# A norm's factor per token taken out of a matmul operand and put on the results, with regrouped convolution taps, in a two-block transformer kernel on one Trainium2 core

## The reference, cut to what matters

```python
def hybrid_layer(x, ...):
    h = rms_norm_2(x, norm_g)            # x * rsqrt(mean(x*x) + eps) per token, times norm_g per channel
    proj = jnp.einsum('bsd,dn->bsn', h, w_in)
    (q_a, k_a, v_a, o_a, i_a, f_a, z_a, c_q, c_kv, k_r, z_b, g_a, g_b) = jnp.split(proj, offsets, axis=-1)
    qk_a = jax.nn.silu(causal_depthwise_conv(jnp.concatenate([q_a, k_a], axis=-1), conv_w))   # 4 taps in time
    h_a = rms_norm(mlstm_chunkwise(q, k, v_a, i_a + gate_bias[:H_A], f_a + gate_bias[H_A:]))
    y_a = (jax.nn.sigmoid(o_a) * h_a * jax.nn.silu(z_a)) @ w_a
    q_b = rms_norm_2(c_q, q_lat_g) @ w_uq;   kv_b = rms_norm_2(c_kv, kv_lat_g) @ w_ukv
    o_b = causal_attention(...)          # k_r, rotated, is shared by all heads
    y_b = (o_b * jax.nn.silu(z_b)) @ w_b
    return x + (jax.nn.sigmoid(g_a) * y_a + jax.nn.sigmoid(g_b) * y_b) @ w_out
```

## Time and profile before

| | |
|---|---|
| time, median of 3 runs | 2551.07 us (2550.17 to 2552.93) |
| profiled execution, its own time | 2552.17 us |
| its span | 2550.4 us |
| mean granted TensorE clock | 0.997 |
| ACT busy | 1250.1 us, 49% |
| DVE busy | 1619.5 us, 63% |
| POOL busy | 146.2 us, 6% |
| chain that ended last | PE 94%, ACT 2%, DVE 2%, DMA 1% |
| loaded from HBM | 506.93 MB, 200 GB/s over the span |

### The profile page before, as it was taken

One profiled execution on the slowest core, in us unless ns is written; L12 is line 12 of the kernel. 1 busy time (PEld: TensorE's weight loads), 2 busy tenths in 40 slices (PEclk: granted clock), 3 DMA queues, 4 the chain that ended last, 5 costly groups with the idle time before them and its releaser, 6 DMA issues.

```text
span 2550.4 us, 34507 instructions
## 1 busy us (share of the span) xinstructions
PE 2514.2 (99%) x13608; PEld 2133.0 (84%) x13608; DVE 1619.5 (63%) x2365; ACT 1250.1 (49%) x1899; POOL 146.2 (6%) x148
## 2 busy tenths in 40 slices
PE   6999999999999999999999999999999999999999
PEld 2688899998888888888888888888888888888887
DVE  3576787886588886566665666665555554545554
ACT  3244433334465554355554555555566665544443
POOL 1001100010001110001110000001000000000000
PEclk8999999999999999999999999999999999999999
DMA  9953677775569885566665455555554555555555
GB/s 334 342 181 114 224 244 248 245 240 184 206 192 273 268 262 190 194 189 189 191 190 191 163 169 174 174 170 185 174 164 151 157 166 189 181 190 184 188 189 165
DMA packets 459104, 511.42 MB, mean 201 GB/s; under 512 B 36771, under 2 KB 327682, under 8 KB 458432
## 3 DMA queue, kind: packets, MB, share of 16 engines
q1 hardware_dynamic: 455936, 501.11, 61.9%
q0 software_dynamic: 2864, 8.11, 1.0%
q10 hardware_dynamic: 144, 0.02, 0.0%
HBM read 506.93 MB, written 2.22 MB: 200 GB/s over the span
## 4 chain that ended last, share of the span: by engine, by line
PE 94%; ACT 2%; DVE 2%; DMA 1%; issue 1%; SPq 0%; DVEq 0%; ACTq 0%
PE PG L926 17%; PE PG L928 17%; PE PG L927 17%; PE PG L916 13%; PE PG L919 6%; PE PG L935 4%; PE PG L937 4%; PE PG L936 4%; PE PS L831 1%; PE PS L1040 1%; ACT wh L1179 1%; PE PG L847 1%; DMA XC<-in_ctxT 1%; PE PS L1104 1%; PE PG L849 1%
## 5 line engine op out<-in xcount | busy, mean ns | idle before, releaser
L1576 DVE TENSOR_TENSOR wl<-raw,wh 128x1024 fp32r<-128x1024 f32 (+1 forms) x745 | 910.3, 1225 | 705.2 <-ACT wh L1179 703.3
L1179 ACT ACTIVATE wh<-raw 128x1024 fp32r<-128x1024 f32 (+1 forms) x745 | 785.9, 1057 | 863.1 <-PE PG L928 575.6
L916 PE MATMUL PG<-FHL,wh 128*128 128x512 f32 x1376 | 431.1, 397 | 2.4 <-DVE UP L1832 1.5
L926 PE MATMUL PG<-wh,HHL 128*128 128x512 f32 x832 | 331.3, 398 | 0.1
L928 PE MATMUL PG<-wl,HHL 128*128 128x512 f32 x832 | 324.9, 391 | 0.0
L927 PE MATMUL PG<-wh,HHL 128*128 128x512 f32 x832 | 324.3, 390 | 0.0
L919 PEld LDWEIGHTS PG<-FHL,wl 128*128 128x128 f32 x1376 | 256.3, 188 | 59.4
L919 PE MATMUL PG<-FHL,wl 128*128 128x256 f32 x1376 | 267.9, 278 | 0.0
L916 PEld LDWEIGHTS PG<-FHL,wh 128*128 128x128 f32 x1376 | 210.8, 189 | 5.2 <-issue 3.7
L928 PEld LDWEIGHTS PG<-wl,HHL 128*128 128x128 f32 x832 | 156.2, 188 | 33.6
L927 PEld LDWEIGHTS PG<-wh,HHL 128*128 128x128 f32 x832 | 156.6, 188 | 30.6
(11 more groups left out here) (402 smaller groups left out, 4222.2 us busy)
## 6 DMA issues: line engine op xcount, KB each, us to landing
raw<-in_w_in SPq DMA_DIRECT2D x208, 512.0 KB, 3.4
raw<-in_w_up SPq DMA_DIRECT2D x344, 256.0 KB, 3.4
raw<-in_w_ada SPq DMA_DIRECT2D x128, 512.0 KB, 5.0
raw<-in_w_down SPq DMA_DIRECT2D x84, 512.0 KB, 3.8
raw<-in_w_qkv SPq DMA_DIRECT2D x80, 512.0 KB, 4.6
first<-in_w_ada SPq DMA_DIRECT2D x78, 256.0 KB, 6.7
raw<-in_w_o SPq DMA_DIRECT2D x32, 512.0 KB, 3.8
raw<-in_w_in SPq DMA_DIRECT2D x64, 256.0 KB, 3.0
```

What stands on the lines that cost most here:

```text
L916: pe.matmul(to, hi[:, 128 * j:128 * j + 128], flat(FHL[:, step.k, :, :]), start=step.first, stop=False, skip_group_check=True)
L926: pe.matmul(dst, xh[:, cols], hi, start=step.first and j % per == 0, stop=False, skip_group_check=True)
L1179: ac.activation(wh[n % NSPL][:, 0:src.shape[1]], src, ACT.Copy).then_inc(S["hi"], 1)
L1576: dv.tensor_tensor(wl[n % NSPL][:, 0:x], src, wh[n % NSPL][:, 0:x], ALU.subtract).then_inc(S["lo"], 1)
```

## The change

The second block's operand is made from x itself, without the factor per token. `scale`, `warm` and the split first chunk go for "h". `turned` of `xh` reads XT and needs only the residual: its pieces 0 to 5 stand in down1 1 to 3, the last two behind steps 3 and 6 of lat 0. `norm` stands behind step 4 of lat 0. The factor is put on the results: for those with tokens on partitions as ScalarE's scale (lat, mv, sig, silu, out, mix, mixb, in two halves where one instruction did both halves of the tokens); for those with channels on partitions (small, mqk) by VectorE with a row of factors RR, which a product of ones with a diagonal matrix spreads over the partitions (`rows_h`). The convolution then works on MSG, the scaled copy of mqk in SBUF, and its taps stand at steps 3, 5, 7 and 8 of mv g, its Silu at step 11. Head 3 of the attention has other places.

```diff
         if g == 1:
-            after, plus = ("k", 2, 0), ((14, 15, 16, 17, 18, 19, 25, 25, 26, 26), (27, 27, 28, 28, 29, 30, 32, 32, 33, 34))
+            after, plus = ("k", 2, 0), ((14, 15, 16, 17, 18, 19, 25, 25, 26, 26), (26, 27, 27, 28, 28, 29, 31, 31, 34, 35))
...
     residual("down1", ("tail2", 0, 0), 0, "h")
-    normed("h", ("tail2", 0, 0), ("lat", 0, 0))
+    P.put(("lat", 0, 0), 4, "norm", "h", 0)
+    for phase, n in enumerate((6, 9, 10)):
+        P.put(("lat", 0, 0), n, "rows_h", 0, phase, phase == 1)
+    for i in range(8):
+        turned("xh", i, ("down1", i // 2 + 1, 0) if i < 6 else ("lat", 0, 0), (5 if i < 6 else 3) + 3 * (i % 2))
...
-    for phase, n in enumerate((0, 1, 2, 8, 9)):
+    for phase, n in enumerate((0, 2, 3, 8, 9)):
         P.put(("mqk", 0, 0), n, "small", 0, phase, phase in (1, 3))
...
     for g in range(4):
+        P.put(("mv", g, 0), 0, "m_conv", g, 6)
         P.put(("mv", g, 0), 0, "m_conv", g, 0)
         for j in range(4):
-            P.put(("mv", g, 0), 1 + j, "m_conv", g, 1 + j)
-        P.put(("mv", g, 0), 6, "m_conv", g, 5)
+            P.put(("mv", g, 0), (3, 5, 7, 8)[j], "m_conv", g, 1 + j)
+        P.put(("mv", g, 0), 11, "m_conv", g, 5)
...
+            elif (job, phase) == ("rows_h", 1):
+                w.wait_ge(S["diag_h"], 1)
+                w.wait_ge(*free(u))
+                pe.matmul(ps[:, 0:T], ones[:, :], flat(DIAGH[:, :, :]), start=True, stop=True).then_inc(S["side"], 1)
...
+                elif name == "xh":
+                    w.wait_ge(S["res"], 2 * nth("res", ("down1", i // 2), 0))
...
-            elif (job, phase) == ("small", 0):
-                w.wait_ge(*product_done("small", 0))
-                ac.activation(KRF[:, :], result("small", 0)[0:64, 0, 0:T], ACT.Copy).then_inc(S["kr_raw"], 1)
+            elif (job, phase) == ("rows_h", 2):
+                u = use("rows_h", 0, 1)
+                w.wait_ge(*full(u))
+                ac.activation(RR[:, :], bank(u)[:, 0:T], ACT.Copy).then_inc(emptying(u), 1)
...
             elif (job, phase) == ("m_conv", 0):
                 g, b = key, key % 2
-                w.wait_ge(*product_done("mqk", g))
+                w.wait_ge(*out_done("mqk", g))
                 if g >= 2:
                     w.wait_ge(*full(use("mlstm", 2 * g - 3, 0, 1)))
                 for j in range(4):
                     ch = 8 * (j // 2) + 2 * g + j % 2
-                    end = ac.activation(MQK[b][:, j, :], result("mqk", g)[:, j // 2, T * (j % 2):T * (j % 2) + T],
-                                        ACT.Identity, scale=cw2[:, 3, ch:ch + 1])
+                    end = ac.activation(MQK[b][:, j, :], MSG[b][:, j, :], ACT.Identity, scale=cw2[:, 3, ch:ch + 1])
...
-                ac.activation(RG[n % 2][:, :, :], result(name, g)[:, :, :],
-                              ACT.Sigmoid if name == "sig" else ACT.Silu).then_inc(out_sem(name, g), 1)
+                for j in range(2):
+                    end = ac.activation(RG[n % 2][:, j, :], result(name, g)[:, j, :],
+                                        ACT.Sigmoid if name == "sig" else ACT.Silu, scale=xr[:, j:j + 1])
+                end.then_inc(out_sem(name, g), 1)
...
             elif (job, phase) == ("small", 0):
                 ps = result("small", 0)
-                dv.tensor_scalar(gates[:, 0, :], ps[64:72, 0, 0:T], gb[:, 0:1], None, ALU.add)
-                w.wait_ge(S["kr_raw"], 1)
-                dv.tensor_scalar(gates[:, 1, :], ps[96:104, 0, 0:T], gb[:, 1:2], None,
-                                 ALU.add).then_inc(out_sem("small", 0), 1)
+                w.wait_ge(*product_done("small", 0))
+                w.wait_ge(*emptied(use("rows_h", 0, 1)))
+                dv.tensor_tensor(KRF[:, :], ps[0:64, 0, 0:T], RR[0:64, :], ALU.mult).then_inc(S["kr_raw"], 1)
+                dv.tensor_tensor(gates[:, 0, :], ps[64:72, 0, 0:T], RR[64:72, :], ALU.mult)
+                dv.tensor_tensor(gates[:, 1, :], ps[96:104, 0, 0:T], RR[96:104, :], ALU.mult).then_inc(c.sem, c.up())
+                w.wait_ge(c.sem, c.n)
+                dv.tensor_scalar(gates[:, 0, :], gates[:, 0, :], gb[:, 0:1], None, ALU.add)
+                dv.tensor_scalar(gates[:, 1, :], gates[:, 1, :], gb[:, 1:2], None, ALU.add).then_inc(out_sem("small", 0), 1)
+            elif (job, phase) == ("rows_h", 0):
+                w.wait_ge(S["xr"], 2)
+                dv.tensor_tensor(DIAGH[:, :, :], ident[:, :].unsqueeze(1).to_broadcast([128, 2, 128]),
+                                 xr[:, :].unsqueeze(2).to_broadcast([128, 2, 128]), ALU.mult).then_inc(S["diag_h"], 1)
+            elif (job, phase) == ("m_conv", 6):
+                g, b = key, key % 2
+                w.wait_ge(*product_done("mqk", g))
+                w.wait_ge(*emptied(use("rows_h", 0, 1)))
+                if g >= 2:
+                    w.wait_ge(S["m_centre"], g - 1)
+                dv.tensor_tensor(MSG[b][:, :, :], result("mqk", g)[:, :, :].rearrange("p a (c n) -> p (a c) n", c=2),
+                                 RR[:, :].unsqueeze(1).to_broadcast([128, 4, T]), ALU.mult).then_inc(out_sem("mqk", g), 1)
...
-                dv.tensor_copy(lr[:, 2 * key:2 * key + 2], y).then_inc(S["lat_r"], 1)
+                dv.tensor_tensor(lr[:, 2 * key:2 * key + 2], y, xr[:, :], ALU.mult).then_inc(S["lat_r"], 1)
...
                     end = dv.scalar_tensor_tensor(
-                        out=MQK[b][:, j, d:T], in0=result("mqk", g)[:, j // 2, T * (j % 2):T * (j % 2) + T - d],
+                        out=MQK[b][:, j, d:T], in0=MSG[b][:, j, 0:T - d],
```

More of the change, by code:

```diff
@@ L583, in build @@
     RT = at("RT", [128, 2, 4, 64], F32, 199)
+    DIAGH = at("DIAGH", [128, 2, 128], F32, 178)
+    RR = at("RR", [128, T], F32, 179)
+    MSG = [at(f"MSG{i}", [128, 4, T], F32, 140 + 4 * i) for i in range(2)]
     KRH = at("KRH", [128, 2, 4, 64], F32, 201)
@@ L1005, in piece @@
             elif job == "warm":
-                p = P.of["up" if key == "f" else "lat", 0]
+                p = P.of["up", 0]
                 t = p + 1
@@ L1349, in piece @@
                 for n in range(2):
-                    end = ac.activation(LJUNK[:, n, :], result("lat", key)[:, n, :], ACT.Square,
+                    end = ac.activation(LJUNK[:, n, :], result("lat", key)[:, n, :], ACT.Square, scale=xr[:, n:n + 1],
                                         accum_out=lss[:, 2 * key + n:2 * key + n + 1])
@@ L1377, in piece @@
                     w.wait_ge(*full(use("mlstm", 2 * key - 3, 4, 1)))
-                ac.activation(MV[key % 2][:, :, :, 0:T], result("mv", key)[:, :, :].rearrange("p j (h e) -> p j h e", h=2),
-                              ACT.Copy).then_inc(out_sem("mv", key), 1)
+                for n in range(2):
+                    end = ac.activation(MV[key % 2][:, n, :, 0:T], result("mv", key)[:, n, :].rearrange("p (h e) -> p h e", h=2),
+                                        ACT.Copy, scale=xr[:, n:n + 1])
+                end.then_inc(out_sem("mv", key), 1)
             elif (job, phase) == ("mlstm", 2):
@@ L1415, in piece @@
                     w.wait_ge(*full(use("turned", ("ha", 7), 0)))
-                ac.activation(cols4(GA if name == "mix" else GB, g), result(name, g)[:, :, :],
-                              ACT.Sigmoid).then_inc(out_sem(name, g), 1)
+                for j in range(2):
+                    end = ac.activation(cols4(GA if name == "mix" else GB, g)[:, j, :], result(name, g)[:, j, :],
+                                        ACT.Sigmoid, scale=xr[:, j:j + 1])
+                end.then_inc(out_sem(name, g), 1)
             elif (job, phase) == ("qr_out", 0):
@@ L1506, in piece @@
                 w.wait_ge(*full(u))
-                if name in ("xf", "xh") and i == 0:
-                    if name == "xf":
-                        w.wait_ge(S["gain"], NCH + 1)
+                if name == "xf" and i == 0:
+                    w.wait_ge(S["gain"], NCH + 1)
                     for k in range(2):
@@ L2059, in piece @@
                 _, dst, _, gain = turns[name]
-                if name in ("xf", "xh") and i == 0:
+                if name == "xf" and i == 0:
                     for k in range(2):
[L2062 to L2071, removed]
+                        w.wait_ge(*((S["xlo"], 1) if k == 0 else (S["xf_hi"], 1)))
+                        dv.tensor_scalar(MTF[0][:, k, :], bank(u + k)[:, 0:T], gain[:, k:k + 1], MOD[:, 3, k:k + 1],
+                                         ALU.mult, ALU.add).then_inc(c.sem, c.up())
+                        w.wait_ge(c.sem, c.n)
+                        dv.tensor_tensor(dst[:, 1, k, :], MTF[0][:, k, :], dst[:, 0, k, :],
+                                         ALU.subtract).then_inc(emptying(u + k), 1)
                     return
```

19 lines of the change are left out of this document (10 added, 9 removed).

## The result

The changed kernel takes 2556.25 us (median of 15 runs, 2555.57 to 2557.02) against 2551.00 of the kernel before, measured beside it: ratio 1.0019, 95% interval 1.0012 to 1.0026. It is slower by 5.2 us, 3 to 7 by the interval, and so at the edge of what was called no change. The forecast had 2552.5, with +1.4.

A forecast was written before the change was run, and what follows sets the result against it. TensorE, busy 2514.2 of 2550.4 us, was taken as the bound. Terms -6.4 + 0.6 + 10.8 - 3.6 = +1.4 gave 2553.6 for a profiled-like execution, 2552.5 for the median; 8-in-10 range 2543.0 to 2559.0, own range 2549 to 2556.

The forecast's parts named there:

- Part 1: Gap between the blocks: lat 0 starts right behind down1, with a new wait of some 0.8 us; -6.4 us.
- Part 2: small: more VectorE work and a later chain of exponentials lengthen TensorE's 1.01 us wait for `wl`; +0.6 us.
- Part 3: Convolution: ScalarE's wait for MSG brings three TensorE waits in each of mv 1 to 3, none in mv 0; +10.8 us.
- Part 4: Attention's fourth head: the 2.88 us wait for PT and its halved clock go, a 0.9 us wait comes; -3.6 us.
- Part 5: 24 ScalarE copies or activations split in halves: 5 us more ScalarE work, each hidden by a whole product; cost 0.
- rival D: The fourth head gains nothing: 2556.1 us; chance 0.08.
- The walk: Step-by-step timing of mv 1 from trace durations: TensorE waits 1.2 for MP, 0.9 at the last tile, 1.5 at mqk 2's first.
- A: Rival: the convolution costs nothing, ScalarE's wait for MSG is made good within two tiles of lead; 2541.7 us; chance 0.20.
- B: Rival: in the convolution only MP is late, the other two waits vanish; 2545.3 us; chance 0.10.
- C: Rival: the new waits also take TensorE's clock; 2557.3 us, or 2558.9 if small's wait does too; chance 0.12.
- E: Rival: the gap between the blocks does not close, lat 0 waits for late chunks or factors; 2558.9 us; chance 0.05.

The follow-up runs named there:

- the faster version: Changed kernel with centre taps at step 2, tap groups at 3, 5, 6, 7, Silu at 9, last residual behind lat 0's first split: 2544.49 us.

## Why the prediction was right, and which terms were off

**Sign and size.** +1.4 was forecast and +5.2 measured, inside the range of 8 in 10, which is 16 us wide. Parts 1, 2 and 3 came as walked; parts 4 and 5 were off, part 4 in a way that also touched the conversion to a median. The 2556.25 lies at the edge of the forecast's own 2549 to 2556 and beside the 2556.1 of rival D; that it hits D's number is chance, for D's cause is not what happened.

**The terms, stretch by stretch.** All kernels run the same product matmuls in the same order, so one and the same matmul can be looked up in two traces. How far its start moves in a stretch is what the change does there. Starts in us:

| in before | in the changed kernel | what lies in the stretch | forecast | measured |
|---|---|---|---|---|
| 0 to 250.09 | 0 to 250.73 | the start | 0 | +0.64 |
| to 301.07 | to 298.53 | part 4, the fourth head | -3.6 | -3.18 |
| to 1000.20 | to 997.54 | nothing changed | 0 | -0.12 |
| to 1500.04 | to 1490.96 | part 1, end of down1 and lat | -6.4 | -6.42 |
| to 1525.06 | to 1516.85 | part 2, and the wait for LTMP | +0.6 | +0.87 |
| to 1570.09 | to 1561.88 | mv 0 | 0 | 0.00 |
| to 1731.20 | to 1733.54 | part 3, mv 1 to 3 | +10.8 | +10.55 |
| to 2101.26 | to 2104.82 | part 5, the halves | 0 | +1.22 |

The sum is +3.6, as between the spans of the two profiled executions. The experiments' traces repeat these figures where they keep the part: part 1 is -6.4, part 2 +0.9 and part 3 between 10.5 and 10.6 in every trace with the changed kernel's places. In the stretch of part 3 the distance to before is 0.0 with the convolution undone, +5.4 with the centre taps at step 2, +0.7 with the Silu at 9 as well and -0.2 in the faster version, where MSG and all its work are kept.

**Part 1** (-6.4). Right, with a slip in the adding that is too small to matter: its terms -7.7, 0.4 and 0.8 make -6.5. The gap closed, and the wait of 0.8 is one of 0.61 in the row.

**Part 2** (+0.6). Right: the wait of 1.01 is 1.70. The other 0.2 of the stretch is the wait for LTMP, which the prediction did not name.

**Part 3** (+10.8). Right in size and mechanism, and not by luck. The walk's waits are distances to the time at which TensorE would have come without a pause, so they compare with the distances of starts, not with the numbers in brackets. Against the trace with the convolution undone, the changed kernel's matmuls in mv 1 fall back by 1.1 at MP, 0.7 at the last tile and 1.6 at the next product's first tile, and nowhere else by more than 0.03. The walk had 1.2, 0.9 and 1.5. The numbers in brackets alone (0.95, 0.45, 1.29) would give 2.7 per mv in place of 3.4.

**Part 4** (-3.6). This failed in size. "It costs 4.5 in all" took the halved clock of one profiled execution for a cost of every execution. In two other traces with the old places, waits of 2.90 and 2.46 left the clock at 1.00, and the stretch is 1.6 and 1.7 shorter than in the trace of before. Against these two the changed kernel's trace gains 1.5, the nine traces with the new places gain 0.7 to 1.6, and the medians give 0.7 to 1.5. The wait that the new places bring was 1.07 for 0.9. The same mistake sat in the last line of the sum: the profiled execution of before stood 1.1 above the median, and the clock's fall, 1.6, was in it. Subtracting 1.1 at the end and crediting the change with the 1.6 counted a delay that the median runs need not have had. Without it part 4 is -2.0, and the forecast by its own terms +3.0.

**Part 5** (0). Wrong in kind. "Each is hidden by a whole product" looked at the PSUM buffer alone. ScalarE's order has more behind a gate's activation than the buffer: the attention's exponentials, for which TensorE already waited 1.7 us. The stretch grows by 1.2, and with the gates and mixes whole it is 0.2 shorter than in before, so the halves cost 1.2 to 1.4; the medians give 1.0 to 1.7.

**The rivals.** A and B are out: rows of MP, `wl` and the next tile are all there. C did not happen in the changed kernel, whose clock stays at 1.00 from 1500 to its last matmul; the doubled MSG shows falls behind waits of 2.2, so C was not far off. D is half right: the gain was about 1.5, neither 3.6 nor 0. E is out. The Trainium skill's case of short idles that swing the clock (TensorE: Matmul & The Clock Gate, section "A second HAM failure mode") is not seen here: nine waits of 0.4 to 1.3 us between 1583 and 1706 left it at 1.00. Whether the falls behind the doubled MSG's single waits of 2.2 are that case no run shows. The Trainium skill's figures for SBUF and PSUM sources on ScalarE (DVE Perf Modes, section "The TRN2 errata") differ by 0.04 us, somewhat more than the centre taps show: a median of 0.495 from SBUF against 0.469 from PSUM.

**The sum, measured.** The table's +3.6 holds the 1.6 of the clock's fall in before as if the change had removed it. Without that it is +5.2, the same as by the medians. That the two agree so closely is in part chance, since the start alone differs by 0.6, and the runs of one kernel differ by 1 to 5 us. Of the 3.8 us between forecast and measurement, 1.6 are the clock, 0.5 the rest of part 4, 1.2 part 5 and 0.2 LTMP; the rest is below what these runs can tell.

## What to carry to other kernels

When an engine walks one fixed order, a new wait costs what is queued behind it, not what it waits for: list the work that feeds the bound engine (here the weight splits) and put the waiting piece behind the next of it. The change's own gain was real, and most of its loss lay in the places of two pieces: moving them turned +5.2 us into -4.9, and with the tap groups and the last residual moved as well it was -7.2, with all the added work kept. A stretch at half clock in one profiled execution may be a chance event until a second trace of the same wait shows it; take it out before a term is sized, and out of the distance to the median too. And where two kernels run the same long list, compare the start of the same instruction in both traces: here that sized terms of 1 us which medians with intervals of 2.5 us to either side could not.

## What the runs showed of the hardware that was not expected

Equal waits do not have equal consequences for TensorE's clock. A wait of 2.88 us at the fourth head is followed by a clock of 0.50 in one trace; waits of 2.90 and 2.46 at the same place left it at 1.00 in two others. Of three waits of 2.2 us in one execution two were followed by a fall, at a cost of 1.7 us each. Past the first 60 us of the execution no wait of up to 1.7 us was, in the traces of both kernels and of ten experiments. Why one wait is followed by a fall and its equal is not, no run here shows.
